# End stage of a one-core layer kernel: five private token tiles, the expert pair summed on TensorE, broadcast rows loaded in earlier stages

## The reference, cut to what matters

```python
# in trunk_layer, x is the residual stream, g2 a row of 1024 gains
h = rms_norm(x, p['norm2_g']) * (1 + sc2) + sh2
x = x + g2 * hier_moe(h, p)          # hier_moe: weighted sum of two expert outputs
# after the layer
y_prompt = rms_norm(xp, final_norm_g)
y_sample = rms_norm(xs, final_norm_g)
```

## Time and profile before

| what | value |
|---|---|
| median of 3 runs | 1311.78 us (1309.76 to 1312.71) |
| the profiled execution's own time | 1309.53 us |
| its span | 1307.7 us |
| PE, DVE, ACT, POOL busy | 919.8, 615.1, 294.1, 89.3 us |
| mean granted TensorE clock | 0.789 of full |

### The profile page before, as it was taken

How to read it: one execution, slowest core, us unless ns; L and a number is a source line. 1 busy time by engine, 2 the same in 40 slices (tenths; PEclk the granted TensorE clock), 3 DMA queues, 4 the chain that set the end, 5 groups by cost and what they waited for, 6 DMA issues and landing times. The chain is left out here.

```text
span 1307.7 us, 15405 instructions
## 1 busy us (share of the span) xinstructions
PE 919.8 (70%) x5907; PEld 578.9 (44%) x5907; DVE 615.1 (47%) x1286; ACT 294.1 (22%) x499; POOL 89.3 (7%) x71
## 2 busy tenths in 40 slices
PE   1699988989368786776867659983047899697710
PEld 1365555666255665665756324452012344242300
DVE  2317999355568676786742432335601111010124
ACT  2230000323525244273211540101000111010102
POOL 0000000010010010100100000001311111111031
PEclk9889999989675575755756779985568999798965
DMA  9835511200110011101140730110359999989543
GB/s 334 291 153 210 196 55 57 75 9 17 17 26 9 10 25 17 26 1 18 25 164 3 276 163 33 49 49 19 147 232 381 394 421 419 377 340 398 193 156 145
DMA packets 72967, 193.72 MB, mean 148 GB/s; under 512 B 42629, under 2 KB 43023, under 8 KB 58687
## 3 DMA queue, kind: packets, MB, share of 16 engines
q1 hardware_dynamic: 64272, 174.05, 35.8%
q0 software_dynamic: 5840, 10.63, 2.1%
q10 hardware_dynamic: 2783, 8.06, 1.7%
HBM read 181.74 MB, written 19.36 MB: 154 GB/s over the span
## 5 line engine op out<-in xcount | busy, mean ns | idle before, releaser
L521 PE MATMUL bank<-arena 128*128 128x320 f32 x704 | 200.8, 445 | 14.3 <-DVE arena L413 6.1
L521 PEld LDWEIGHTS bank<-arena 128*128 128x128 f32 x704 | 135.3, 194 | 81.5 <-issue 30.0
L1998 PE MATMUL bank<-arena 128*64 128x512 f32 (+2 forms) x528 | 131.0, 668 | 34.7 <-DMA arena<-in_expert_w_up 33.6
L921 DVE SCALAR_TENSOR_TENSOR arena<-arena 128x655 f32<-128x655 f32 x116 | 104.7, 902 | 4.6 <-DVE arena L921 0.2
L1998 PEld LDWEIGHTS bank<-arena 128*64 128x64 f32 (+2 forms) x528 | 45.7, 151 | 118.3 <-issue 116.9
L1466 PE MATMUL bank<-arena 128*128 128x512 f32 x160 | 78.6, 655 | 11.6 <-issue 11.6
L2079 DVE TENSOR_TENSOR arena<-arena,bank 128x256 f32<-128x256 f32 x17 | 7.2, 422 | 161.6 <-ACT arena L2053 161.6
L2020 PE MATMUL bank<-arena 128*64 128x512 f32 (+2 forms) x264 | 62.4, 599 | 9.9 <-DVE arena L2082 9.9
L883 ACT ACTIVATE arena<-bank 64x128 f32<-64x128 f32 (+1 forms) x68 | 19.9, 292 | 170.7 <-PE bank L1256 169.4
L1466 PEld LDWEIGHTS bank<-arena 128*128 128x128 f32 x160 | 33.4, 211 | 54.2 <-issue 54.2
L1984 PE MATMUL bank<-arena 128*128 128x128 f32 x136 | 19.7, 290 | 52.9 <-DMA arena<-tokens_for_experts,arena 52.9
(11 more groups left out here) (309 smaller groups left out, 1440.9 us busy)
## 6 DMA issues: line engine op xcount, KB each, us to landing
arena<-in_expert_w_gate SPq DMA_DIRECT2D x33, 1024.0 KB, 14.4
arena<-in_expert_w_up SPq DMA_DIRECT2D x33, 1024.0 KB, 17.2
arena<-in_expert_w_down SPq DMA_DIRECT2D x33, 1024.0 KB, 18.3
arena<-in_ada_w SPq DMA_DIRECT2D x12, 2048.0 KB, 10.2
arena<-in_w_in SPq DMA_DIRECT2D x22, 512.0 KB, 3.7
arena<-expert_rows SPq DMA_DIRECT2D x10, 512.0 KB, 8.4
arena<-in_x_sample SPq DMA_DIRECT2D x8, 512.0 KB, 7.7
arena<-in_w_out SPq DMA_DIRECT2D x1, 4096.0 KB, 14.7
```

The source lines that it names most:

```text
L521: mm = nc.tensor.matmul(psum[4 + 2 * (n % 2) + half][:, 0:HALF], wring[:, n % NWIN, k], hT[:, k, half * HALF:(half + 1) * HALF], start=(k ...
L921: chain(nc.vector.scalar_tensor_tensor(acc, src, w, acc, ALU.mult, ALU.add))
L1998: mm = nc.tensor.matmul(psum[2 + n % 2][r, :], xeT[:, n % 2, c, r], gu[:, :, c, :], start=(c == 0), stop=(c == KD - 1))
```

## The change

Five buffers of `ya` and of `yb` instead of three, in the space of expert buffers 3 and 4. No tile's load waits for a store any more. The pair is no longer added by GpSimd: PE multiplies each half row of `ya` and of `yb` by the identity matrix into one PSUM bank, and DVE's gain product reads PSUM, in two halves of 512 columns. The transfers of `g2b` move to the output stage, behind `norm2_g` and ahead of the first expert loads; that of `fgain` moves into the expert stage, behind the loads of the fourth expert and ahead of the wait for the table. The stores share one semaphore.

```diff
@@ sp_out
             sp.dma_start(h2, ins["norm2_g"].broadcast_to([P, D])).then_inc(s_modb, 16)
+            for c in range(2):
+                sp.dma_start(g2b[:, c], modrows[c:c + 1, 5 * D:6 * D].broadcast_to([P, D])).then_inc(s_fg, 16)
@@ regions
-        rege = Region(zbase, wbase)
-        NF = 3
-        ya, yb = rege.take(NF, D), rege.take(NF, D)
-        g2b, fgain, fsq = rege.take(2, D), rege.take(D), rege.take(D)
+        rege = Region(ebuf[NB - 1])
+        ya, yb = rege.take(TILES, D), rege.take(TILES, D)
+        fsq = rege.take(D)
+        g2b, fgain = regp.take(2, D), regm.take(D)
@@ sp_end, pe_end (new)
         def sp_end():
             sp = nc.sync
-            for c in range(2):
-                sp.dma_start(g2b[:, c], modrows[c:c + 1, 5 * D:6 * D].broadcast_to([P, D])).then_inc(s_fg, 16)
-            sp.dma_start(fgain, ins["final_norm_g"].rearrange("(o n) -> o n", o=1).broadcast_to([P, D])
-                         ).then_inc(s_fg, 16)
             for i in range(TILES):
-                if i >= NF:
-                    sp.wait_ge(s_fst[i % NF], 16 * (i // NF))
                 for k, dst in enumerate((ya, yb)):
-                    sp.dma_start(dst[:, i % NF], yexp[k * T + i * P:k * T + (i + 1) * P, :]).then_inc(s_fin_in[i % NF], 16)
+                    sp.dma_start(dst[:, i], yexp[k * T + i * P:k * T + (i + 1) * P, :]).then_inc(s_fin_in[i], 16)
+
+        def pe_end():
+            pe = nc.tensor
+            for i in range(TILES):
+                pe.wait_ge(s_fin_in[i], 32)
+                if i >= 2:
+                    pe.wait_ge(s_ymul, i - 1)
+                for h in range(2):
+                    half = slice(512 * h, 512 * h + 512)
+                    nc.tensor.matmul(psum[2 * (i % 2) + h][:, :], ident, ya[:, i, half], start=True, stop=False)
+                    mm = nc.tensor.matmul(psum[2 * (i % 2) + h][:, :], ident, yb[:, i, half], start=False, stop=True)
+                mm.then_inc(s_ysum, 1)
@@ dve_end
-                y = ya[:, i % NF]
+                y = ya[:, i]
                 dve.wait_ge(s_ysum, i + 1)
-                chain(nc.vector.tensor_tensor(y, y, g2b[:, int(i > 0)], ALU.mult))
+                chain(nc.vector.tensor_tensor(y[:, 0:512], psum[2 * (i % 2)][:, :], g2b[:, int(i > 0), 0:512], ALU.mult))
+                chain.announce(nc.vector.tensor_tensor(y[:, 512:D], psum[2 * (i % 2) + 1][:, :],
+                                                       g2b[:, int(i > 0), 512:D], ALU.mult), s_ymul, i + 1)
                 chain.announce(nc.vector.tensor_tensor(x2[:, i], x2[:, i], y, ALU.add), s_xf, i + 1)
@@ act_end, pool_end
-                act.dma_start(tok_dst(i), ya[:, i % NF]).then_inc(s_fst[i % NF], 16)
-            for b, stored in enumerate(s_fst):
-                act.wait_ge(stored, 16 * len(range(b, TILES, NF)))
-
-        def pool_end(chain):
-
-            pool = nc.gpsimd
-            for i in range(TILES):
-                pool.wait_ge(s_fin_in[i % NF], 32 * (i // NF + 1))
-                chain.announce(nc.gpsimd.tensor_tensor(ya[:, i % NF], ya[:, i % NF], yb[:, i % NF], ALU.add),
-                               s_ysum, i + 1)
-
+                act.dma_start(tok_dst(i), ya[:, i]).then_inc(s_fst, 16)
+            act.wait_ge(s_fst, 16 * TILES)
@@ SP's order
             for n in range(2, 4):
                 experts_load(n)
+            sp.dma_start(fgain, ins["final_norm_g"].rearrange("(o n) -> o n", o=1).broadcast_to([P, D])
+                         ).then_inc(s_fg, 16)
             sp.wait_ge(s_ovst, 1)
             sp.wait_ge(s_tab, 16)
@@ order of the other engines
-            pool_end(chain)
...
+            pe_end()
```

More of the change, by code:

```diff
@@ L1658, in build @@
         s_escat = [sem(f"expert_out_scattered{b}") for b in range(2)]
-        s_fst = [sem(f"final_stored{b}") for b in range(NF)]
+        s_fst = sem("final_stored")
         s_et, s_eTa, s_eTd = (sem(n) for n in (
@@ L1664, in build @@
             "expert_out_low", "expert_out_high"))
-        s_fin_in = [sem(f"rows_back{b}") for b in range(NF)]
+        s_fin_in = [sem(f"rows_back{i}") for i in range(TILES)]
+        s_ymul = sem("expert_sum_scaled")
         s_ysum = sem("two_experts_summed")
```

## The result

The changed kernel takes 1296.44 us (median of 4 runs, 1295.17 to 1298.88); the kernel before, run beside it and counted with its earlier runs, 1310.77 (1307.41 to 1312.71). The ratio is 0.9902, interval [0.9873, 0.993]. In a later comparison, of five rounds, it was 1298.9 against 1306.45, ratio 0.994 [0.9918, 0.9962]. The forecast was 1297.1.

A forecast was written before the change was run, and what follows sets the result against it. End stage bound by first-row latency, a vector chain and two buffer waits. Tile 0's final product 7.3 us earlier (5.9 - 1.5 + 2.9) plus 7.4 from later tiles gave 14.7 us: 1297.1 from median 1311.78, range 1292 to 1302.

The forecast's parts named there:

- First rows: End stage: without three broadcast transfers ahead, the first pair of rows lands earlier, so the start is 5.9 us earlier.
- VectorE's work: End stage: a 1.23 us gain product becomes two of 0.693 from PSUM; a residual takes 2.71 us instead of 2.52.
- TensorE's sum: End stage: four products per tile take 1.90 us at full clock, 3.81 at half; half taken for tiles 0 and 1.
- Two residuals beside GpSimd: End stage, tiles 0 and 1: residuals took 9.09 us beside GpSimd's adds, now 6.19 with the wait; 2.9 saved.
- the kindred case: Rival counted with slow rows: landing transfers, not GpSimd, stretch VectorE's additions; 4.0 us more, 1301.1; joint chance 0.04.
- No wait for buffers: End stage, after tile 0's final product: no store is waited for; three steps take 14.4 us instead of 21.8, 7.4 saved.
- The moved transfers: Output and expert stages: `g2b` costs nothing there; `fgain`, behind experts 2 and 3, taken as nothing by a free stretch.
- the rival's lower end: Expert stage: `fgain` delays the table or first gather by 1.3 to 2.7 us, total 1298.4 to 1299.8; chance 0.11.
- signs of failure: Rows over 5.3 us apart, VectorE held by store or sums after tile 1, or table to last scatter over 3 us longer.
- full clock from the start: Rival, end stage: TensorE at full clock from its first sum, 2.7 us less, 1294.4; chance 0.14.
- slow rows: Rival, end stage: rows land at 197 GB/s, 4.8 us more, 1301.9; chance 0.04 together with stretched additions.
- a slip of the expert stage: Rival, expert stage: shifted loads miss freed buffers and TensorE's weight waits grow; at 20 us growth 1317; chance 0.02.

The follow-up runs named there:

- `fgain` last: The changed kernel with the `fgain` transfer put back at the end, ahead of the rows: stage 45.01 us, median 1300.63 us, ratio 0.9932 to the kernel before.

## Why the prediction was right, and where it was not

- **What bounds the end stage** was right in kind. The first rows, moved alone, gave 5.5 us of the 5.8 by which they came earlier. The buffers alone gave 6.1, not the 8.0 of the two idle stretches, since GpSimd then stretched one operation more. The vector chain alone, with the sum on TensorE, gave nothing: that stage grew by 4.5 us.
- **First rows.** 4.8 us after SP's first issue were forecast, 4.95 came; 5.9 us saved were forecast, 5.8 measured (10.71 to 4.95). Shown by the run with that part alone and, from the other side, by `fgain` last.
- **VectorE's work.** 0.69 us for a product from PSUM, 4.79 between final products: both to the hundredth.
- **TensorE's sum: the step that failed.** "A tile takes 3 x 0.435 + 0.59 = 1.90" and at half clock 3.81. The pace was right, the count was not: a product of fp32 operands is two instructions of the record, so a tile is eight and not four. The row that I used showed it: line 1466 has x160, for five tiles of two banks and eight products each, which are 80 calls. By count it is 7 x 0.87 + 1.20 = 7.3 us cold and 7 x 0.435 + 0.59 = 3.6 warm; measured were 6.49 (the clock rises on the way) and 3.81, from the first instruction to VectorE's start. I had 3.91 for the cold one. That is 2.6 us of the stage's 42.5 - 39.6 = 2.9; the rest is the last tile, 4.13 us instead of 3.76 (below).
- **Half or full clock** was rightly chosen, and the gap between them, forecast at 2.7 us, measured 2.7, but again for other counts: the sum at full clock took what I had given for half.
- **Two residuals beside GpSimd** gained what was said, and the kindred case against it, that landing rows stretch VectorE, is out by the run with five buffers. What the prediction didn't see is that this gain and the cost of TensorE's sum cancel: without TensorE's sum the stage is the same, 42.48 us.
- **No wait for buffers**: 7.4 forecast; from first to fourth final product 21.77 us became 14.35.
- **The moved transfers: a term set at nothing that was not nothing.** `g2b` cost nothing that a trace shows. `fgain` was set at nothing, "by the nearest row, that free stretch"; it costs the table's load 1.5 us, the rival's lower end. The free stretch was real but began at 952, while the table's load had stood on the chain since 949.8. So `fgain` didn't fall beside free engines but lengthened the traffic at whose end that load lands. That it costs the load about 1.5 us is shown by taking it away; that it does so by the end of the traffic is read from the twelve traces. How much of it reaches the end of the kernel is not shown.
- **The total.** By the stage and the table, if all of the table's part reaches the end, the gain is 11.7 - 1.5 = 10.2 us, not 14.7. The two comparisons gave 14.3 and 7.6 us between medians, with intervals that both hold 10.2. In the profiled pair the 14.5 us are 5.9 + 11.7 - 3.2: the changed kernel had its slot entries landed 5.9 us earlier, and it was 5.7 ahead already before the first instruction that the change adds (the loads of the modulation rows are issued at 728.57 instead of 734.30); from the landing of the slot entries to that of the last scatter it took 3.2 us longer, 1.5 of them in the table's load. That the time was met within 1 us was luck, and it doesn't prove a ledger.
- **The signs.** One of the prediction's own signs of failure came: the stretch from the start of the table's load to the last scatter's landing grew from 303.7 to 306.9 us, by 3.2 where 3 was the limit; from the load's landing it grew by 1.7. From the landing of the slot entries, kernels without `fgain` there took up to 307.5, so what exceeds the load's 1.5 us is within their variation.

The rivals: full clock from the start did not occur; slow rows did not (377 to 442 GB/s); no gain at all and a slip of the expert stage that eats the gain did not. TensorE waited for expert weights as before, five times and 33.8 us against 33.6 in the earlier trace rows.

## What to carry to other kernels

Before pricing an added instruction by a row, divide that row's count by the number of calls in the source: a call may be more than one instruction. Where TensorE had been idle for 10.8 to 18.0 us here, it did the first 3.5 to 6 us of its work at half clock, so let the engine that stands waiting do the first tiles itself and bring in the other where its start is covered. The slot table, a small load on the chain, landed in all twelve profiles only when the long queue beside it had run dry, so look at what is added to such a queue, not only at where it ends. Judge an edit in a stage by the stage's own length in the trace; here it repeats within 1 us, while the time of the whole moves by several.

## What was not expected of the hardware

A broadcast from DRAM just ahead of the rows ran at 164 to 262 GB/s in the earlier trace rows, and six like it in the output stage, queued behind other loads, at some 390 to 430. With `fgain` last one transfer of 0.52 MB delayed the rows by 2.3 us, which is some 230 GB/s. Part of it is the start: in the changed kernel the rows alone began with slices of 131, 197 and 238 GB/s too, before they reached 393. Why the rate stays low for longer behind a broadcast here, and not in the output stage, stays open; it was not tried further.

In the last tile the reciprocal waits 0.77 us for the root in the changed kernel and 0.40 in the four kernels whose sum is on GpSimd. It is 0.77 too with TensorE's sum and three buffers, so it goes with that sum, not with the buffers. The cause stays open; the price is 0.37 us.
